# Seven products instead of eight for the output projection of a hybrid attention layer, with the weight sums made on the way

## The reference, cut to what matters

```python
h = rmsnorm(x, norm_g)
proj = h @ w_in
...
mixed = jnp.concatenate([o_gla, o_pool, o_mem], axis=-1)
x = x + mixed @ w_out
return rmsnorm(x, final_g)
```

## Time and profile before

| | |
|---|---|
| median of 3 runs | 1374.05 us |
| the profiled execution | 1374.18 us |
| its span, first to last instruction | 1372.5 us |
| TensorE busy | 98% of the span |
| VectorE, ScalarE, GpSimd busy | 62%, 57%, 27% |
| DMA: moved, mean rate | 269.33 MB, 196 GB/s |

### The profile page before, as it was taken

One profiled execution on the slowest core, in us unless ns is written; L12 is line 12 of the kernel. 1 busy time (PEld: TensorE's weight loads), 2 busy tenths in 40 slices (PEclk: granted clock), 3 DMA queues, 4 the chain that ended last, 5 costly groups with the idle time before them and its releaser, 6 DMA issues.

```text
span 1372.5 us, 35662 instructions
## 1 busy us (share of the span) xinstructions
PE 1348.6 (98%) x14763; PEld 1013.7 (74%) x14763; DVE 845.0 (62%) x1600; ACT 785.2 (57%) x1449; POOL 371.8 (27%) x313
## 2 busy tenths in 40 slices
PE   6999999999999999999999999999999999999998
PEld 5788668576695968869586785958769596886954
DVE  6876667576556655565665655565565655556456
ACT  7896545655546465564656645464564646556353
POOL 2120164135322142332223323132332214233100
PEclk9999999999999999999999999999999999999999
DMA  9576556663673737556383654737466373755631
GB/s 385 191 215 209 209 184 228 193 244 135 203 258 89 277 114 261 185 183 232 98 304 120 236 214 134 267 93 274 158 204 258 93 273 112 261 185 183 237 95 56
DMA packets 143768, 269.33 MB, mean 196 GB/s; under 512 B 75152, under 2 KB 88720, under 8 KB 140432
## 3 DMA queue, kind: packets, MB, share of 16 engines
q1 hardware_dynamic: 142912, 266.20, 56.5%
q10 hardware_dynamic: 720, 1.06, 0.2%
HBM read 220.03 MB, written 30.41 MB: 182 GB/s over the span
## 4 chain that ended last, share of the span: by engine, by line
PE 94%; DVE 3%; ACT 1%; DMA 1%; issue 0%; SPq 0%; ACTq 0%; DVEq 0%
PE bank L683 34%; PE bank L722 33%; PE bank L701 10%; PE bank L917 2%; PE bank L943 2%; PE bank L937 2%; PE bank L1003 2%; PE bank L1035 1%; PE bank L928 1%; PE bank L958 1%; PE bank L804 1%; PE bank L901 1%; DMA out_parts<-fg 1%; DVE arena L1655 1%; PE bank L788 1%; PE bank L952 1%
## 5 line engine op out<-in xcount | busy, mean ns | idle before, releaser
L683 PE MATMUL bank<-ring,arena 128*128 128x512 f16 x1440 | 318.6, 380 | 0.0
L683 PEld LDWEIGHTS bank<-ring,arena 128*128 128x128 f16 x1440 | 138.4, 98 | 165.4 <-issue 5.9
L722 PE MATMUL bank<-arena,ring 128*128 128x128 f16 x4032 | 237.1, 219 | 0.0
L722 PE MATMUL bank<-arena,wres 128*128 128x128 f16 x4032 | 237.0, 219 | 0.0
L722 PEld LDWEIGHTS bank<-arena,ring 128*128 128x128 f16 x4032 | 228.4, 98 | 5.2 <-DVE arena L1633 1.8
L722 PEld LDWEIGHTS bank<-arena,wres 128*128 128x128 f16 x4032 | 227.7, 98 | 2.5 <-issue 2.5
L683 PE MATMUL bank<-wv,arena 128*128 128x512 f16 x768 | 168.5, 379 | 0.2 <-DVE wv L1619 0.2
L2157 POOL TENSOR_TENSOR arena<-arena 128x1024 f32<-128x1024 f32 (+2 forms) x42 | 64.8, 1543 | 352.9 <-ACT arena L1093 350.7
L683 PEld LDWEIGHTS bank<-wv,arena 128*128 128x128 f16 x768 | 75.0, 98 | 87.9 <-DVE wv L1619 0.4
L2165 POOL TENSOR_TENSOR arena<-arena 128x1024 f16<-128x1024 f32 x32 | 67.6, 2136 | 195.1 <-ACT arena L1111 182.4
L701 PE MATMUL bank<-arena,wres 128*128 128x256 f16 x768 | 86.1, 273 | 0.1
(11 more groups left out here) (274 smaller groups left out, 2090.2 us busy)
## 6 DMA issues: line engine op xcount, KB each, us to landing
ring<-out_parts SPq DMA_DIRECT2D x120, 512.0 KB, 5.4
ring<-gate_parts SPq DMA_DIRECT2D x92, 512.0 KB, 5.9
ring<-side_parts SPq DMA_DIRECT2D x92, 512.0 KB, 6.2
arena<-in_xt SPq DMA_DIRECT2D x16, 1024.0 KB, 6.4
arena<-in_x SPq DMA_DIRECT2D x32, 512.0 KB, 4.3
out<-arena SPq DMA_DIRECT2D x31, 512.0 KB, 2.9
arena<-in_w_out SPq DMA_DIRECT2D x16, 512.0 KB, 5.5
out_parts<-arena SPq DMA_DIRECT2D x6, 512.0 KB, 6.9
```

Of the source, the lines that this page charges most:

```text
L683: mm = nc.tensor.matmul(ap, lhs, rhs, start=k == 0 and n == 0, stop=(k, n) == last)
L722: mm = nc.tensor.matmul(ap, w[:, p, k, j * P:(j + 1) * P], x_part(r, b)[:, k, :], start=fresh and j == 0 and k == 0 and n == 0, stop=k == ...
```

## The change

**Seven products for the output projection of blocks 6 to 13**, made in the steps 7 to 14 (`is_seven`). `mixed` and `w_out` are each cut in two by two: tokens in tiles of 128, columns and rows in halves of 512. In place of four quarters of 24 matmuls there are seven products of 12, each between one combination of blocks of `mixed` and one combination of blocks of `w_out` (`out_seven`): 84 matmuls of 128x512 instead of 96. The products go to banks 0, 1 and 6; VectorE adds them with nine additions (`add_seven`) instead of four.

**Sums of `mixed`.** GpSimd makes them in `mixed_sums`, ScalarE and VectorE split them (`split_hi`, `split_lo`).

**Sums of `w_out`**, made once, in the steps 3 to 6 (`makes_sums`), a quarter in each: SyncE loads two row tiles (`pair_in`), ScalarE scales them (`pair_scaled`), GpSimd makes the four sums (`out_sums`), ScalarE and VectorE split them (`sums_hi`, `sums_lo`), SyncE stores them to DRAM (`sums_out`, 1 MB).

**Loads and stores.** In the steps 7 to 14 SyncE loads 14 slots for the output instead of 8, and its order is another: loads for a product stand ahead of the transposes. The first token tile of the output has its own buffer, `y0`. These steps keep the residual out of the queue until the projections are done.

**VectorE.** `add_11(GG)` stands ahead of the scans (from step 4 on), and the multiplication of the pool heads (`pool_gate`) ahead of the last additions in the steps 7 to 14. The steps 4 to 6 are written out; the loop of VectorE, ScalarE and GpSimd now starts at step 7.

The diff, cut to its core:

```diff
+SEVEN = 7
+T2, T1, T4, T3 = range(4)
+OUT_BANK = (0, 1, 0, 1, 6, 0, 1)
+OUT_SLOT = ((7, 2), (3, 4), (5, 6), (0, 1), (2, 7), (3, 4), (5, 6))
+OUT_SPLIT = (1, 1, 2, 1, 3, 3, 1)
...
+        def makes_sums(i):
+            return isinstance(i, int) and WHOLE - 1 <= i < SEVEN
...
+            def pair_in(i):
+                k = sum_row(i)
+                if is_whole(i):
+                    sp.wait_ge(lo_c, COMBINED + len(MADE))
+                else:
+                    sp.wait_ge(ad[PM], 4 * (i + 1))
+                    sp.wait_ge(q_ok, 2 * (i + 1))
+                    sp.wait_ge(qm_lo, 2 * (i + 1))
+                for n in range(2):
+                    sp.dma_start(wpair[n].rearrange("p h c -> p (h c)"), w_out[:, k + 4 * n, :]).then_inc(d_wot[n], 16)
...
+            def sums_out(i):
+                k = sum_row(i)
+                sp.wait_ge(lo_o, KT + 2 * k + 2)
+                sp.dma_start(sums_d[:, :, k // 2, :, k % 2, :], wsum).then_inc(d_wot[2], 16)
...
+                    sum_in(2, T2, 1)
+                    sp.wait_ge(pe_f[PM], 3 * i + 1)
+                    to_slot(7, wo_d[:, 0, 0, :, :, :].rearrange("p r k c -> p (r k c)"))
+                    sums_in(3, T1)
+                    sp.wait_ge(pe_f[PM], 3 * i + 2)
+                    to_slot(2, wo_d[:, 0, 1, :, :, :].rearrange("p r k c -> p (r k c)"))
+                    quads_in(1, 0, 1)
+                    sp.wait_ge(pe_f[PM], 3 * i + 3)
+                    sum_in(2, T2, 0)
+                    residual_seven(i, 0)
+                    sp.wait_ge(pe_out, out_made(i) + 1)
+                    quads_in(4, 1, 1)
+                    turn(i, 0)
+                    turn(i, 1)
+                    sp.wait_ge(pe_out, out_made(i) + 2)
+                    sums_in(5, T3)
+                    residual_seven(i, 1)
+                    turn(i, 2)
+                    turn(i, 3)
+                    sp.wait_ge(pe_out, out_made(i) + 3)
+                    sums_in(6, T4)
+                    sp.wait_ge(pe_out, out_made(i) + 4)
+                    gates_in((0, 1))
+                    sp.wait_ge(pe_out, out_made(i) + 5)
+                    gates_in((2,))
+                    sides_in((0,))
+                    sp.wait_ge(pe_out, out_made(i) + 6)
+                    gates_in((3, 4))
+                    store(i - 1, 0)
+                    sp.wait_ge(pe_out, out_made(i) + 7)
+                    gates_in((5, 6))
+                    sp.wait_ge(d_store, 16 * (2 * i - 1))
+                    store(i - 1, 1)
+                    return
...
                 for n in range(4):
                     turn(i, n)
+                if makes_sums(i):
+                    sums_out(i)
                 store(i - 1, 0)
                 residual(i - 1, 1)
...
+            def out_seven(i, n):
+                pe.wait_ge(m_hi, mixed_split(i) + OUT_SPLIT[n])
+                pe.wait_ge(m_lo, mixed_split(i) + OUT_SPLIT[n])
+                if n in (2, 3, 5):
+                    pe.wait_ge(y_add, rows_added(i) + {2: 1, 3: 2, 5: 3}[n])
+                if n == 4:
+                    pe.wait_ge(sT_ok, 2 * i + 2)
+                if n == 6:
+                    pe.wait_ge(y_add, rows_added(i) + 8)
+                for s in OUT_SLOT[n]:
+                    pe.wait_ge(d_slot[s], 16 * loads("out" if n < 4 else "more", i, s))
+                first, t = 4 * (n in (1, 5, 6)), n in (3, 6)
+                for k in range(4):
+                    w = ring[:, OUT_SLOT[n][k // 2], :].rearrange("p (r k c) -> p r k c", r=2, k=2)
+                    for m, (p, r) in enumerate(((0, 0), (0, 1), (1, 0))):
+                        lhs = s2hl[:, p, k, :] if n == 2 else mhl[:, p, first + k, t * P:(t + 1) * P]
+                        mm = nc.tensor.matmul(bank[OUT_BANK[n]][:, :], lhs, w[:, r, k % 2, :],
+                                              start=n not in (2, 5) and k == 0 and m == 0, stop=k == 3 and m == 2,
+                                              skip_group_check=True)
+                mm.then_inc(pe_out, 1)
...
+            def pair_scaled(i):
+                k = sum_row(i)
+                for n in range(2):
+                    act.wait_ge(d_wot[n], 32 + 16 * (k + 1))
+                    nc.scalar.activation(wpair[n], wpair[n], ACT.Copy,
+                                         scale=o_gain[:, k + 4 * n:k + 4 * n + 1]).then_inc(hi_o, 1)
+            def sums_hi(i):
+                k = sum_row(i)
+                act.wait_ge(xn_ok, 2 * (i + 2))
+                act.wait_ge(cb_ok, 16 + 4 * (k + 1))
+                for n in range(2):
+                    nc.scalar.activation(wsum[:, 2 * n:2 * n + 2, 0, :],
+                                         wpair[n], ACT.Copy).then_inc(hi_o, 1)
...
-                    norm_y(i - 1, 0)
+                if is_seven(i, last):
+                    x_plain(i + 1)
+                    norm_y(i - 1, 0, rows_added(i) + 5, y0)
+                elif not first:
+                    if makes_sums(i):
+                        sums_hi(i)
+                    norm_y(i - 1, 0, rows_added(i) + 2)
+                if makes_sums(i):
+                    x_plain(i + 1)
...
+            def sums_lo(i, n):
+                k = sum_row(i)
+                dve.wait_ge(hi_o, KT + 4 * k + 3 + n)
+                nc.vector.tensor_tensor(wsum[:, 2 * n:2 * n + 2, 1, :], wpair[n], wsum[:, 2 * n:2 * n + 2, 0, :],
+                                        ALU.subtract).then_inc(lo_o, 1)
...
+            def add_seven(i, m):
+                t, h, b, made, before = (None, (0, 0, 0, 1, 0), (0, 0, 1, 2, 1), (0, 1, 0, 3, 0), (0, 1, 1, 4, 3),
+                                         (0, 1, 6, 5, 4), (1, 0, 0, 6, 0), (1, 1, 0, 6, 0), (1, 1, 1, 4, 7),
+                                         (1, 0, 1, 7, 6))[m]
+                if m in (1, 6):
+                    dve.wait_ge(d_res, 16 * (2 * i - 1 + t))
+                if m == 1:
+                    dve.wait_ge(sc_ok, i)
+                dve.wait_ge(pe_out, out_made(i) + made)
+                if before:
+                    dve.wait_ge(y_add, rows_added(i) + before)
+                row = (y0, yb)[t][:, h * 512:h * 512 + 512]
+                nc.vector.scalar_tensor_tensor(row, bank[b][:, :], sc_out, row, ALU.mult, ALU.add).then_inc(y_add, 1)
...
-                if not first:
-                    norm_rows(i - 1, 0)
+                if is_seven(i, last):
+                    add_seven(i, 4)
+                    add_seven(i, 5)
+                    pool_gate()
+                    add_seven(i, 6)
+                    add_seven(i, 7)
+                    add_seven(i, 8)
+                    norm_rows(i - 1, 0, rows_added(i) + 5, y0)
+                elif not first:
+                    norm_rows(i - 1, 0, rows_added(i) + 2)
+                if makes_sums(i):
+                    sums_lo(i, 0)
+                    sums_lo(i, 1)
                 if not last:
                     dve.wait_ge(xn_ok, 2 * (i + 2))
...
+            def out_sums(i):
+                k = sum_row(i)
+                (b11, b12), (b21, b22) = [[wpair[n][:, h, :] for h in range(2)] for n in range(2)]
+                pool.wait_ge(hi_o, KT + 4 * k + 2)
+                nc.gpsimd.tensor_tensor(b22, b22, b12, ALU.subtract).then_inc(cb_ok, 1)
+                nc.gpsimd.tensor_tensor(b12, b12, b11, ALU.subtract).then_inc(cb_ok, 1)
+                pool.wait_ge(cb_ok, 16 + 4 * k + 1)
+                nc.gpsimd.tensor_tensor(b11, b22, b11, ALU.add).then_inc(cb_ok, 1)
+                pool.wait_ge(cb_ok, 16 + 4 * k + 3)
+                nc.gpsimd.tensor_tensor(b21, b21, b11, ALU.subtract).then_inc(cb_ok, 1)
...
+            def mixed_sums(i):
+                made = 3 * (i - SEVEN)
+                pool.wait_ge(mmax_ok, i)
+                pool.wait_ge(bl_ok, i + 1)
+                pool.wait_ge(x_lo, x_base(i) + XPARTS)
+                nc.gpsimd.tensor_tensor(mixed[:, 0:4, P:TB], mixed[:, 0:4, P:TB], mixed[:, 4:8, P:TB],
+                                        ALU.add).then_inc(ms_ok, 1)
+                pool.wait_ge(ms_ok, made + 1)
+                nc.gpsimd.tensor_tensor(sg[0], mixed[:, 0:4, P:TB], mixed[:, 0:4, 0:P], ALU.subtract).then_inc(ms_ok, 1)
+                pool.wait_ge(ms_ok, made + 2)
+                pool.wait_ge(d_store, 16 * (2 * i - 2))
+                nc.gpsimd.tensor_tensor(s43.rearrange("p (b k) t -> p b k t", b=2),
+                                        mixed[:, 4:8, :].rearrange("p k (b t) -> p b k t", b=2),
+                                        sg[0].unsqueeze(1).broadcast_to([P, 2, 4, P]), ALU.subtract).then_inc(ms_ok, 1)
...
+                if makes_sums(n - 1):
+                    out_sums(n - 1)
+                    pool.wait_ge(lo_o, KT + 2 * sum_row(n - 1) + 2)
                 x_plain(n)
```

213 lines of the change are left out of this document (164 added, 49 removed).

## The result

The changed kernel takes 1390.69 us (median of 4 runs, 1386.63 to 1391.44) against 1373.78 us; the ratio is 1.0113, with an interval of 1.010 to 1.0126. The forecast was 1368.7 us and a range up to 1381: wrong in sign and by 22 us. The profiled execution took 1391.12 us, its span is 1389.2 us.

A forecast was written before the change was run, and what follows sets the result against it. TensorE, busy 81.47 of 81.47 us in step 9, was taken as the bound. 1374.18 us less 20.7 (matmuls) plus 15.3 (stalls) gave 1368.8, 1368.7 us for the median; range 1359 to 1381 us.

The forecast's parts named there:

- What goes: Steps 7 to 14: TensorE does 84 matmuls in place of 96, 2.59 us less in each step, 20.7 us in all.
- The chain of the steps 3 to 6: Making and storing the sums delays the residual's reload; TensorE stalls before QK phase 0, 3 x 4.0 + 3.3 = 15.3 us.
- point 7: Steps 3 to 6: store(i-1, 0), issued behind the sums at 849.3, lands 1.3 us after them, at 854.3.
- Rival A: The chain in steps 3 to 6 is short: stalls of 5.7 us in all, 1359 us; chance 0.17.
- Rival C: Stalls in steps 3 to 6 also lower TensorE's clock: 2 us more, four times, 1377 us; chance 0.14.
- I cost all this at 0, with cover of 0.4 to 1.0 us: Steps 7 to 14: added loads, additions, sums and splits make TensorE wait nowhere, being 0.4 to 1.0 us in time.
- Rival B: Steps 7 to 14: weights of products 5 and 6 arrive late, 1.3 us a step, 1379 us; chance 0.16.
- Rival D: Something hidden, such as head_ms waiting for the heads' squares, replaces the saving in the products: 1389 us; chance 0.03.

The follow-up runs named there:

- experiment 6: Kernel before, one VectorE reduction added ahead of the fourth addition in steps 4 to 14, three sizes: 1385.78, 1411.97 and 1452.81 us for waits of 0.93, 2.00, 5.20 us.
- Experiment 5: Changed kernel with the seven products divided over the four places as 2, 2, 1, 2 instead of 2, 2, 2, 1 in steps 7 to 14: 1387.05 us.
- experiments 1: Changed kernel with the store of the sums issued behind the store of rows and the residual's reload in steps 3 to 6: 1372.17 us.
- 2: Changed kernel with VectorE's first norm_rows moved behind its last addition in steps 7 to 14: 1392.26 us.

## Why the prediction was wrong, step by step

- **What goes**: right. Seven products are 84 matmuls, and 2.59 us of TensorE's work went from each of eight steps.
- **The chain of the steps 3 to 6**: right in mechanism, place and nearly in size, 17.1 us for 15.3. `sums_out` went out 2.3 us behind the end of `norm_rows` (2.8 predicted), and the store behind it reported after 6.7 us and not after 2.6, which was point 7. Too small was the landing of the sums (4.8 to 6.2 us; 4.4 predicted). The 3.1 us from `rows(2)` to the end of `rows(3)` were 2.7 in two steps and 3.4 and 3.6 in the two others. Rival A is out. The rule of the Trainium skill that was cited there ("DMA: Bandwidth & Descriptors", "Queues, rings and completion order") is in agreement with the trace: in all four steps the store reported 1.2 to 1.3 us behind the sums.
- **Rival C, the clock, happened**, at the size that its text gave: 8 us there, 7.9 us measured. That the sums agree so closely is luck, since the four losses were between 1.6 and 2.6 us. It was held to be another case with a chance of 0.14, with the argument that TensorE came from 80 us of full work. That argument is what failed. Rows 13 showed half speed behind 3.5 us of idle time, and no row showed a full clock behind such a wait; experiment 6 has it 11 times in 11 behind 5.2 us, each time out of full work. Waits of 3.13 and 3.16 us escaped it in other runs, so it was not certain for each; but a forecast of four waits of 3 to 4 us had to contain this cost. The Trainium skill's rule ("TensorE: Matmul & The Clock Gate", "What's actually happening") that half rate is the default agrees with the trace here too: 22 matmuls of 128x128 in 2 us right behind the wait.
- **"I cost all this at 0, with cover of 0.4 to 1.0 us"**: this is the step that was wrong in kind. It checked each product of TensorE for its inputs up to the end of the step, and `head_ms`, and stopped there. Six of the seven products stand ahead of the heads' last stage and one behind it, so the saved matmuls came out of the 5.3 us that the earlier trace rows show at 849.99, between the heads and the next step. What VectorE, ScalarE and GpSimd do behind the heads did not become shorter (GpSimd's last sums began 6.8 us behind their first matmul before, 7.4 us after) and lost 2.6 us of room. GpSimd fell into the time of the gated heads, VectorE took up to 1.0 us longer for one of them, and TensorE waited 0.8 us for the low-rank product, 6.4 us in all. Experiment 5 shows it: with the products at another place, and all the other work still done, that wait is gone.
- The Trainium skill ("SBUF — State Buffer", "SBUF: two separate sides") says that a VectorE operation with two inputs in SBUF and a GpSimd operation that reads SBUF shut each other out, for the whole instruction. The trace agrees: L2243, both inputs in SBUF, takes 0.69 us alone and 1.04 to 1.68 us beside GpSimd, while L2245, with one input in PSUM, keeps its 0.69 us. GpSimd's L2452 at 878.55 keeps its 1.16 us and ends at 879.71, and the L2243 beside it ends 0.54 us later, at 880.25, as if it had begun only then. The second L2243 ends 0.54 us behind L2508 in the same way. The trace of the kernel before already shows the price: in its steps 2 and 3 L1996 took 2.04 to 2.12 us three times, beside GpSimd's sums of 128x1024.
- **Rival B** happened at one of its two products and in two of eight steps of the profiled execution: 3.0 us for the 10.4 that it gave. There the two loads landed after 7.3 and 6.9 us, in the other six steps after 4.4 to 5.4. Product 5 was in time, as worked out. In both steps the DMA engines stood nearly still for about a microsecond just then (12 and 7 GB/s in the two half microseconds from 786.5 us on, 20 and 8 from 1109.0 us on); what stopped them is open. Since the profiles of the experiments 1, 2 and 5 have no such wait, the 1.0 us of cover that the prediction worked out for product 6 was mostly enough, and these 3.0 us are no fixed cost of the change.
- **Rival D** did not happen.

With C inside the forecast (1368.7 + 7.9), the waits at their size (+1.8), and what was missed in the other steps (6.4 + 3.0 + 3.0), the sum is 1390.8 us, against 1391.1 in the profiled execution, from which these terms are read. Two terms failed most: the clock, left out of the forecast (7.9 us), and the room behind the heads, put at 0 (6.4 us). The chances were spread as if the cases excluded each other; stall, clock and late weights add up, and all of them had the same sign.

What stays open: why the products 2 to 5 take 0.14 us longer than the two quarters did, why the DMA engines stood still, and why a wait of 2.00 us takes the clock down in some steps and not in others.

## What to carry to other kernels

When work leaves the bounding engine, ask from between which two hand-overs it leaves: everything that the other engines do between those two has lost that much room. Here 12 matmuls taken from the place with the least room cost 6.4 us of waits, and moving 12 others there gave 5.4 us back. On an engine that never waits, a wait of 2 us or more has to be priced with the lower clock that can follow it (here 1.6 to 2.8 us each time; it came behind all 29 waits above 3.2 us, behind 11 of 16 of 2.0 to 2.1 us, and behind neither of two between them), one below 1.1 us not. And a store that nobody awaits soon goes into the queue behind the transfers that somebody does; here two lines in another order were worth 18.5 us. A wait that stands in one profiled execution should also be looked for in those of near kernels before it is called a cost of the change.
